# A new order of block two's projection, its indexer columns first, and 28 unit turns ahead of seven norms

## The chip, the cores and the metric

The kernel runs as one program on one core of a Trainium2 chip. The metric is the device time of one execution in microseconds, the median of three runs; beside it stands one profiled execution. The engines are TensorE (PE, its weight loads are PEld), VectorE (DVE), ScalarE (ACT), GpSimd (POOL) and SyncE (SP), which issues the loads from DRAM. Each runs its own list of instructions in order and waits for the others by semaphores. Matmuls write to eight banks of PSUM, each of 512 f32 columns; the other engines read them from there.

## The reference

Two transformer blocks of two layers each work on 256 rows of width 1024, in f32. Block one (attention with a context of 256 rows, a Fourier mix, a gated unit, then a squared-ReLU MLP) is not changed, apart from turns added ahead of three of its norms. Block two's attention is what the tables reorder:

```python
h = rms_norm_2(x, attn_norm_g[l])
proj = h @ w_in[l]
(mq, mk, mv, dq, dk, dv, sq, sk, sv, iq, ik, iw) = jnp.split(proj, offsets, axis=-1)
moba = moba_attention(qk(mq, MOBA_HEADS, qg[0]), qk(mk, MOBA_HEADS, kg[0]), split_heads(mv, MOBA_HEADS))
dq_h = qk(dq, 2 * DIFF_HEADS, qg[1])
dk_h = qk(dk, 2 * DIFF_HEADS, kg[1])
...
diff = diff_attention(dq_h[:, 0::2], dq_h[:, 1::2], dk_h[:, 0::2], dk_h[:, 1::2],
                      split_heads(dv, DIFF_HEADS), lam)
diff = rms_norm_2(diff, diff_subln_g[l]) * (1.0 - lam_init)
iq_h = apply_rope(split_heads(iq, IDX_HEADS), cos, sin)
ik_r = apply_rope(ik, cos, sin)
dsa = dsa_attention(qk(sq, DSA_HEADS, qg[2]), qk(sk, DSA_HEADS, kg[2]),
                    split_heads(sv, DSA_HEADS), iq_h, ik_r, iw * (IDX_HEADS ** -0.5))
mix = jnp.concatenate([merge_heads(moba), merge_heads(diff), merge_heads(dsa)], axis=-1)
x = x + mix @ w_out[l]
h2 = rms_norm_2(x, ffn_norm_g[l])
x = x + (jax.nn.silu(h2 @ w_gate[l]) * (h2 @ w_up[l])) @ w_down[l]
```

Here `qk` is a norm over each head of 64 and a rotation (rope). With 256 rows, moba is plain causal attention with 4 heads; differential attention has 4 heads with two score maps each; the sparse attention (dsa) keeps for each query the 64 best causal keys by an indexer score, a weighted sum over 8 heads of relu(iq . ik).

## The kernel before

**Weights.** Every weight passes through slots of 128 x 1024 f32. SP loads a slot into one of 8 raw buffers (`put`, from L706); ScalarE casts it to the rounded type fp32r (L962, `w_hi`), VectorE subtracts to get the rest (L1270, `w_lo`), and PE multiplies it in three matmuls, hi x hi, hi x lo and lo x hi (`three`, L1762). SP may be 8 slots ahead, the casts and splits 4. Activations are split in the same way.

**Norms.** Ahead of a projection VectorE and ScalarE norm the rows, PE turns them (a transpose, a matmul against the unit matrix) into PSUM (`turn_x` in block one, `norm2` in block two, L1867), VectorE and ScalarE write the halves `act_hi` and `act_lo`, and PE starts on the projection. There are eight such norms, the first at the program's start. PE has nothing else to do in them.

**Block two's projection** (`rows2`, L2167) runs over eight blocks of columns in the order of `BLOCKS2`: dq, dk (differential queries and keys, 512 columns each), iq (indexer queries, 512), dv (512), ik (72 columns: the indexer's 64 key columns and 8 weights, one slot with all 8 tiles of k), mqk, sqk (queries and keys of moba and of dsa) and mv_sv (256 columns of moba's values and 256 of dsa's, fetched by two loads a slot). All but ik have four slots with two tiles of k, so there are 29 slots or steps. Behind each step all engines look in the table `FILL2` and do what stands there for this step; behind the slots of the output projection `out2` (8 slots, `down`, L2085) they look in `OUT2`. The entries are:

- ("drain", j, t): ScalarE copies row tile t of block j out of PSUM, with squares for the head norms where there are any.
- ("first", r), ("second", r), ("turn", r): unit r is 256 columns of rotated heads. VectorE does the head norm's sum and the rope in the first half; POOL makes the power -1/2; VectorE scales in the second; PE turns the result in four matmuls (L1908) into bank 2.
- ("score", j), ("weigh", j), ("mix", j): step j of 16 attention steps. PE's scores with the mask (L2033, L2036), then VectorE's maximum (L1586), ScalarE's exponential and VectorE's division (L1597 to L1604); PE turns the probabilities (L2047, "weigh") and multiplies by the values (L2068, "mix"). Steps 0 to 7 are differential (group 0 and 1), 8 to 11 moba (group 2), 12 to 15 dsa (group 3).
- ("logits", g): PE's indexer logits (into bank 2), ScalarE's relu, VectorE's weighted sum. ("search", t, n): n of the 8 rounds (L1730, L1731) in which VectorE finds the 64 best keys of row tile t, eight a round; the last round also writes the mask `seen` (L1734, L1735), without which PE can't score group 3.
- ("square" and "norm", t), ("turn_rows", t): the norm of the differential result, then its turning by PE (L2080).

The table is written by hand: nothing moves by itself, and each engine takes its part of an entry in the table's order. Bank 2 is shared by the units' turns, the logits and the turned rows; `turn_bank` waits for its last reader.

Of the kernel before, what the change touches and what calls it, by code (L numbers as in the profile page):

```python
# [14 lines left out]
P = 128  # L15
D = 1024
KT = D // P
# [8 lines left out]
SPLIT2, MIXES = 6, 6  # L26
W = 512
# [70 lines left out]
def build(nc, A, consts, out, n):  # L98
    top = ExitStack()
    with top:  # L100
# [76 lines left out]
        with ExitStack() as s:  # L177
# [106 lines left out]
        BLOCKS2 = (("dq", DQ), ("dk", DK), ("iq", IQ), ("dv", DV), ("ik", IK), ("mqk", MQ), ("sqk", SQ), ("mv_sv", MV))  # L284
# [38 lines left out]
            4: [("first", 0)],  # L323
            5: [("second", 0), ("first", 1), ("turn", 0)],
            6: [("second", 1), ("turn", 1)],
            7: [("drain", 1, 0), ("drain", 1, 1)],
            8: [("first", 2)],
            9: [("second", 2), ("first", 3), ("turn", 2)],
            10: [("second", 3), ("turn", 3)],
            11: [("drain", 2, 0), ("drain", 2, 1), ("score", 0)],  # L330
            12: [("weigh", 0), ("first", 4), ("second", 4), ("score", 1)],
            13: [("weigh", 1), ("first", 5), ("second", 5), ("score", 2)],
            14: [("weigh", 2), ("turn", 4), ("score", 3)],
            15: [("drain", 3, 0), ("weigh", 3), ("drain", 3, 1), ("turn", 5), ("score", 4)],
            16: [("weigh", 4), ("mix", 0), ("mix", 1), ("drain", 4, 0), ("drain", 4, 1), ("score", 5)],
            17: [("weigh", 5), ("mix", 2), ("mix", 3), ("first", 6), ("second", 6), ("index_scale",), ("turn", 6), ("score", 6)],
            18: [("weigh", 6), ("mix", 4), ("logits", 0), ("logits", 1), ("score", 7)],
            19: [("weigh", 7), ("mix", 5), ("mix", 6), ("logits", 2)],
            20: [("drain", 5, 0), ("drain", 5, 1), ("mix", 7), ("logits", 3)],
            21: [("logits", 4), ("first", 7), ("square", 0)],  # L340
            22: [("logits", 5), ("second", 7), ("first", 8), ("turn", 7), ("square", 1)],
            23: [("second", 8), ("turn", 8), ("norm", 0), ("search", 0, 2)],
            24: [("drain", 6, 0), ("drain", 6, 1), ("search", 0, 3), ("norm", 1), ("turn_rows", 0), ("score", 8)],
            25: [("weigh", 8), ("search", 0, 3), ("turn_rows", 1), ("first", 9), ("score", 9)],
            26: [("weigh", 9), ("second", 9), ("first", 10), ("turn", 9), ("score", 10)],
            27: [("weigh", 10), ("second", 10), ("turn", 10), ("search", 1, 2), ("score", 11)],
            28: [("drain", 7, 0), ("weigh", 11), ("drain", 7, 1), ("search", 1, 1), ("score", 12)],
        }
        OUT2 = {
            0: [("weigh", 12), ("mix", 8), ("mix", 9), ("search", 1, 2), ("score", 13)],  # L350
            1: [("weigh", 13), ("mix", 10), ("mix", 11), ("search", 1, 3), ("score", 14)],
            2: [("weigh", 14), ("score", 15)],
            3: [("weigh", 15), ("mix", 12), ("mix", 13)],
            4: [("mix", 14)],
# [132 lines left out]
        def units2(l):  # L487
            out_ = []
            for name, c, p0, g, q in (("dq", DQ, 4, 2, 1), ("dq", DQ + 256, 6, 2, 1), ("dk", DK, 8, 3, 0), ("dk", DK + 256, 10, 3, 0),
# [1789 lines left out]
```

## Time and profile before

| what | value |
|---|---|
| median of three runs | 1750.43 us (1750.07 to 1750.53) |
| the profiled execution | 1748.0 us |
| its span, first to last instruction | 1745.9 us |
| busy PE, VectorE, ScalarE, POOL | 1614.8, 1049.1, 731.8, 99.2 us |
| mean granted clock of PE | 0.965 |
| read from DRAM | 255.15 MB, 147 GB/s over the span |
| chain that ended last | PE 81%, VectorE 11%, issue 3%, ScalarE 2% |

The span's times start at its first instruction. The granted clock is given as a share: 1.00 is 2.4 GHz, 0.50 is 1.2 GHz. Busy times of PE are modelled: matmuls overlap, so the distance from one start to the next is the better price of one in a row. Block one takes the span up to 964, block two's first layer from there to 1356, the second the rest.

### The profile page before, as it was taken

The numbers are of one execution on the slowest core, as the hardware profiler recorded it, in microseconds if no ns is written. First come the engines' busy times: TensorE is split into PE (matmuls) and PEld (weight loads), VectorE is DVE, ScalarE is ACT, GpSimd is POOL, SyncE is SP. The second block draws the span as 40 slices with busy tenths as digits, with TensorE's granted clock in tenths as the row PEclk, the third lists the DMA queues.
The fourth block names the chain that finished last, engine by engine and source line by source line (L and its number), as shares of the span: only waits on it lengthen the run. The fifth ranks groups of instructions, "written<-read, shape, count | busy, mean of one in ns | idle before, by whom it ended". The sixth has DMA issues, their size and how long they took to land.

```text
span 1745.9 us, 22902 instructions
## 1 busy us (share of the span) xinstructions
PE 1614.8 (92%) x9050; PEld 1309.9 (75%) x9050; DVE 1049.1 (60%) x1599; ACT 731.8 (42%) x1246; POOL 99.2 (6%) x88
## 2 busy tenths in 40 slices
PE   6999889999999989989999897789999887789999
PEld 3865676788888866569988675579998666579997
DVE  3537654533443356666644867758874767768873
ACT  3425523421342224635533544444443444444542
POOL 1010000000000001000000301000000201000000
PEclk9999999999999989999999989899999999899999
DMA  9348224432333324848666632246656432246653
GB/s 358 111 154 312 101 89 135 131 96 89 94 97 95 97 72 133 290 131 268 182 191 184 173 108 83 67 122 183 187 185 189 134 109 83 72 124 186 185 183 119
DMA packets 174218, 257.69 MB, mean 148 GB/s; under 512 B 10448, under 2 KB 92640, under 8 KB 173984
## 3 DMA queue, kind: packets, MB, share of 16 engines
q1 hardware_dynamic: 171872, 250.38, 45.9%
q0 software_dynamic: 2016, 5.77, 1.3%
q8 instruction: 72, 1.18, 0.3%
q14 instruction: 34, 0.28, 0.1%
q10 hardware_dynamic: 224, 0.07, 0.0%
HBM read 255.15 MB, written 1.05 MB: 147 GB/s over the span
## 4 chain that ended last, share of the span: by engine, by line
PE 81%; DVE 11%; issue 3%; ACT 2%; DMA 1%; POOL 1%; SPq 0%; POOLq 0%; DVEq 0%; ACTq 0%
PE bank L1764 49%; PE pair_bank L1764 20%; DVE w_lo L1270 2%; PE bank L1816 2%; PE bank L2015 1%; PE pair_bank L1987 1%; PE pair_bank L2033 1%; PE bank L1998 1%; DVE wide L1354 1%; PE bank L1928 1%; DVE rope_a L1420 1%; POOL xrstd L848 1%; DVE head_sq L1428 1%; DMA raw<-in_w_ada 1%; DVE proj L1448 1%
## 5 line engine op out<-in xcount | busy, mean ns | idle before, releaser
L1270 DVE TENSOR_TENSOR w_lo<-raw,w_hi 128x1024 fp32r<-128x1024 f32 x374 | 450.1, 1219 | 304.8 <-ACT w_hi L962 301.9
L962 ACT CAST w_hi<-raw 128x1024 fp32r<-128x1024 f32 x374 | 386.7, 1044 | 391.1 <-PE bank L1764 315.2
L1764 PE MATMUL pair_bank<-act_hi,w_hi 128*128 128x256 f32 (+1 forms) x736 | 230.4, 313 | 9.9 <-DVE act_lo L1344 4.5
L1764 PE MATMUL pair_bank<-act_hi,w_lo 128*128 128x256 f32 (+1 forms) x736 | 227.0, 308 | 0.0
L1764 PE MATMUL pair_bank<-act_lo,w_hi 128*128 128x256 f32 (+1 forms) x736 | 226.8, 308 | 0.0
L1764 PE MATMUL bank<-w_hi,act_hi 128*128 128x512 f32 (+2 forms) x528 | 218.2, 413 | 4.2 <-DVE w_lo L1270 2.2
L1764 PE MATMUL bank<-w_hi,hid_lo 128*128 128x512 f32 x560 | 221.4, 395 | 0.0
L1764 PE MATMUL bank<-w_hi,hid_hi 128*128 128x512 f32 x560 | 221.3, 395 | 0.0
L1764 PE MATMUL bank<-w_lo,hid_hi 128*128 128x512 f32 x560 | 221.3, 395 | 0.0
L1764 PE MATMUL bank<-w_lo,act_hi 128*128 128x512 f32 (+2 forms) x528 | 209.8, 397 | 0.0
L1764 PE MATMUL bank<-w_hi,act_lo 128*128 128x512 f32 (+2 forms) x528 | 208.9, 396 | 0.0
L1764 PEld LDWEIGHTS pair_bank<-act_hi,w_hi 128*128 128x128 f32 x736 | 140.2, 190 | 25.2 <-DVE act_lo L1344 7.8
L1764 PEld LDWEIGHTS pair_bank<-act_lo,w_hi 128*128 128x128 f32 x736 | 140.2, 190 | 7.4 <-issue 1.0
L1764 PE MATMUL bank<-act_hi,w_hi 128*128 128x256 f32 (+1 forms) x480 | 145.0, 302 | 0.6 <-DVE w_lo L1270 0.6
L1764 PEld LDWEIGHTS pair_bank<-act_hi,w_lo 128*128 128x128 f32 x736 | 140.2, 191 | 7.0
L1764 PE MATMUL bank<-act_hi,w_lo 128*128 128x256 f32 (+1 forms) x480 | 144.3, 301 | 0.0
L1764 PE MATMUL bank<-act_lo,w_hi 128*128 128x256 f32 (+1 forms) x480 | 144.3, 301 | 0.0
L1764 PEld LDWEIGHTS bank<-w_hi,act_hi 128*128 128x128 f32 x528 | 106.9, 202 | 27.6 <-issue 3.4
L1764 PEld LDWEIGHTS bank<-w_hi,hid_lo 128*128 128x128 f32 x560 | 105.1, 188 | 25.4
L1764 PEld LDWEIGHTS bank<-w_hi,hid_hi 128*128 128x128 f32 x560 | 105.2, 188 | 25.3
L1764 PEld LDWEIGHTS bank<-w_lo,hid_hi 128*128 128x128 f32 x560 | 105.1, 188 | 25.3
L1764 PEld LDWEIGHTS bank<-w_hi,act_lo 128*128 128x128 f32 x528 | 105.4, 200 | 21.7
(227 smaller groups left out, 2103.9 us busy)
## 6 DMA issues: line engine op xcount, KB each, us to landing
raw<-in_w_mlp SPq DMA_DIRECT2D x128, 512.0 KB, 3.7
raw<-in_w_ada SPq DMA_DIRECT2D x96, 512.0 KB, 5.7
raw<-in_w_in SPq DMA_DIRECT2D x72, 512.0 KB, 3.6
raw<-in_w_gate SPq DMA_DIRECT2D x44, 512.0 KB, 3.7
raw<-in_w_up SPq DMA_DIRECT2D x44, 512.0 KB, 3.7
raw<-in_w_down SPq DMA_DIRECT2D x44, 512.0 KB, 3.5
raw<-in_w_out SPq DMA_DIRECT2D x32, 512.0 KB, 3.8
raw<-in_w_in SPq DMA_DIRECT2D x16, 256.0 KB, 3.0
```

The source lines that it names most:

```text
L848: nc.gpsimd.tensor_tensor(xrstd[:, m, g:g + 1], xvar[:, m, g:g + 1], neg_half[:, 0:1], ALU.pow).then_inc(xrstd_ready, 1)
L962: nc.scalar.copy(hi_of(i)[:, 0:w], raw[:, i % RAW, 0:w]).then_inc(hi_ready, 1)
L1270: nc.vector.tensor_tensor(w_lo[:, i % RAW, 0:w], raw[:, i % RAW, 0:w], hi_of(i)[:, 0:w].bitcast(F32), ALU.subtract).then_inc(lo_ready, 1)
L1354: nc.vector.tensor_scalar(wide[:, (2 * k + s) % 4, :], b[:, (k % 2) * NT:(k % 2 + 1) * NT], mscale[:, which, k, s:s + 1], mod[:, 24 * whic ...
L1420: nc.vector.tensor_tensor(t1, x, u["cos"].unsqueeze(2).broadcast_to([P, TT, heads, DH]), ALU.mult).then_inc(dve_order, 1)
L1428: ins = nc.vector.tensor_tensor(t2[:, :, :, lo:lo + wd], x[:, :, :, other:other + wd], sin[:, :, lo:lo + wd].unsqueeze(2).broadcast_to([P, ...
L1448: ins = nc.vector.tensor_tensor(d, t1, f, ALU.mult) if u["normed"] else nc.vector.tensor_tensor(d, t1, t2, ALU.add)
L1764: ins = nc.tensor.matmul(o, a[x], b[y], start=first and i == 0, stop=True, skip_group_check=True)
L1816: ins = nc.tensor.matmul(bank[bk][j:j + 32, :], cond[:, k, :], tiles(raw[:, r, :], 2)[:, kk, :], start=k < 4, stop=True, skip_group_check= ...
L1928: ins = nc.tensor.matmul(bank[5][:], proj1[:, 2 * s + t, F1 + i * P:F1 + (i + 1) * P], dft_n[:, t, :], start=t == 0, stop=t == TT - 1)
L1987: nc.tensor.matmul(bank[a][:, 0:w], st["q"][a], st["k"][a], start=True, stop=True).then_inc(scored, 1)
L1998: ins = nc.tensor.matmul(st["o"][a], st["v"][a][kt], probs_t1[:, j % 2, a, kt, :], start=kt == 0, stop=kt == keys - 1)
```

## The change

There are two edits, independent of each other.

**The order.** `BLOCKS2` starts with the indexer queries, then comes a new block mv_ik of 328 columns (moba's 256 values and the indexer's 72 columns) in three slots of 3, 3 and 2 tiles of k, and the last block sv holds only dsa's 256 values, in two slots of 4 tiles. There are 29 slots as before. `FILL2` and `OUT2` are written anew for this order: the indexer's units, the logits and the search start earlier, the attention steps later (the first score stands behind step 17 in place of step 11, the last behind slot 3 of the output projection in place of 2), and the steps come closer together. The units are renumbered, indexer first (`units2`), the banks of the output projection are swapped to fit (`down_bank`), and the buffers of the casts rotate over six from block two's first slot on (`hi_of`, `hi_before`).

**The turns.** `keep_busy` issues 28 turns of the unit matrix into bank 7, which nobody reads, on PE alone. It is called ahead of the turns of `norm2` (four times in a run), of `rows1` in layer 1, and of `up1`'s first slot in layers 0 and 1.

```diff
-SPLIT2, MIXES = 6, 6
+SPLIT2, MIXES, BUSY = 6, 6, 28
...
-        BLOCKS2 = (("dq", DQ), ("dk", DK), ("iq", IQ), ("dv", DV), ("ik", IK), ("mqk", MQ), ("sqk", SQ), ("mv_sv", MV))
+        BLOCKS2 = (("iq", IQ), ("mv_ik", IK), ("dq", DQ), ("dk", DK), ("dv", DV), ("mqk", MQ), ("sqk", SQ), ("sv", SV))
...
-            11: [("drain", 2, 0), ("drain", 2, 1), ("score", 0)],
-            12: [("weigh", 0), ("first", 4), ("second", 4), ("score", 1)],
...
+            24: [("weigh", 6), ("mix", 5), ("second", 7), ("square", 0), ("first", 8), ("turn", 7), ("score", 7)],
+            28: [("drain", 7, 0), ("weigh", 10), ("mix", 9), ("drain", 7, 1), ("second", 9), ("first", 10), ("norm", 1), ("turn", 9), ("score", 11)],
...
         OUT2 = {
-            0: [("weigh", 12), ("mix", 8), ("mix", 9), ("search", 1, 2), ("score", 13)],
...
+            0: [("weigh", 11), ("mix", 10), ("second", 10), ("turn_rows", 0), ("turn", 10), ("turn_rows", 1), ("score", 12)],
...
         def down_bank(key, gs, ch, g):
             if key == "out2":
-                return bank[(4, 2, 5, 3)[2 * ch + g - 2]]
+                return bank[(4, 5, 3, 2)[2 * ch + g - 2]]
...
-            return [(j, name, c, 1 if name == "ik" else 4, KT if name == "ik" else 2, IN2 - IK if name == "ik" else W)
-                    for j, (name, c) in enumerate(BLOCKS2)]
+            shape = dict(mv_ik=(256 + IN2 - IK, (3, 3, 2)), sv=(256, (4, 4)))
+            return [(j, name, c, *shape.get(name, (W, (2, 2, 2, 2)))) for j, (name, c) in enumerate(BLOCKS2)]
...
+                        if name == "mv_ik":
+                            self.put("w", nk * wd, lambda r: [(tiles(r[:, 0:nk * wd], nk)[:, :, 0:256], src[:, ks, MV:MV + 256]),
+                                                              (tiles(r[:, 0:nk * wd], nk)[:, :, 256:wd], src[:, ks, IK:IN2])])
...
-                        if t == 0 and u["r"] >= 2:
+                        if t == 0:
                             self.e.wait_ge(rows_ready, n.at("rows_ready", us[u["r"] - 2]["key"]))
...
+            def keep_busy(self):
+
+                if 7 in self.ada_before:
+                    self.e.wait_ge(mod_ready, n.at("mod_ready", self.ada_before[7]))
+                for i in range(BUSY):
+                    nc.tensor.transpose(bank[7][:, i % 4 * P:(i % 4 + 1) * P], ident, ident)
...
             def norm2(self, m, l, which):
                 e = self.e
+                self.keep_busy()
...
+                if l:
+                    self.keep_busy()
                 for s in both if l else ():
                     self.turn_x(m, both, s, 0)
...
+                        if (h, j, q) == (0, 0, 0):
+                            self.keep_busy()
...
                 if key == "out2":
                     e.wait_ge(drained, n.at("drained", ("rows2", l, 6, 1)))
-                    self.turn_bank()
...
-                        if key == "out2" and ch and j == start:
-                            e.wait_ge(drained, n.at("drained", ("rows2", l, 7, g - 2)))
+                        if key == "out2" and j == start:
+                            if (ch, g) in ((0, 3), (1, 2)):
+                                e.wait_ge(drained, n.at("drained", ("rows2", l, 7, ch)))
+                            elif ch:
+                                self.turn_bank()
```

**Order of instructions.** On PE ahead of block two's first norm, before (`hid` is the last projection of block one, `xn` the normed rows, `const` the unit matrix):

```order
L1764 MATMUL bank<-w_lo,hid_hi 128x512
L1764 MATMUL bank<-w_hi,hid_lo 128x512
L1867 MATMUL pair_bank<-const,xn 128x128 [waits xn_ready]
L1867 MATMUL pair_bank<-const,xn 128x128 x7
L1867 MATMUL bank<-const,xn 128x128 x4
L1867 MATMUL pair_bank<-const,xn 128x128 [waits norm_lo]
L1867 MATMUL pair_bank<-const,xn 128x128 x3
L1764 MATMUL bank<-w_hi,act_hi 128x512 [waits norm_lo,lo_ready]
```

and after:

```order
L1762 MATMUL bank<-w_lo,hid_hi 128x512
L1762 MATMUL bank<-w_hi,hid_lo 128x512
L1826 MATMUL bank<-const 128x128 [waits mod_ready]
L1826 MATMUL bank<-const 128x128 x27
L1873 MATMUL pair_bank<-const,xn 128x128 [waits xn_ready]
L1873 MATMUL pair_bank<-const,xn 128x128 x7
L1873 MATMUL bank<-const,xn 128x128 x4
L1873 MATMUL pair_bank<-const,xn 128x128 [waits norm_lo]
L1873 MATMUL pair_bank<-const,xn 128x128 x3
L1762 MATMUL bank<-w_hi,act_hi 128x512 [waits norm_lo,lo_ready]
```

The 28 turns stand between the last matmul of the MLP and the wait for the normed rows; the norm's own turns and their waits are the same.

On PE in block two's layer 0, where the indexer's keys are projected, before (behind an attention step's turned probabilities, a unit's turns and the next step's scores):

```order
L2047 MATMUL bank<-const,probs 128x128 [waits prob_ready,prob_t]
L1908 MATMUL bank<-const,proj 128x128 [waits rows_ready,turned_out]
L1908 MATMUL bank<-const,proj 128x128 x3
L2033 MATMUL pair_bank<-pairs_t 128x256 [waits exped,turned_out]
L2033 MATMUL pair_bank<-pairs_t 128x256
L2036 MATMUL pair_bank<-mask_b,ident_b 128x128 x2
L1764 MATMUL bank<-w_hi,act_hi 128x72 [waits drained,lo_ready]
L1764 MATMUL bank<-w_lo,act_hi 128x72
L1764 MATMUL bank<-w_hi,act_lo 128x72
```

and after, behind the last slot of iq:

```order
L1762 MATMUL bank<-w_lo,act_hi 128x512
L1762 MATMUL bank<-w_hi,act_lo 128x512
L1762 MATMUL bank<-w_hi,act_hi 128x328 [waits lo_ready]
L1762 MATMUL bank<-w_lo,act_hi 128x328
L1762 MATMUL bank<-w_hi,act_lo 128x328
```

The matmuls of 72 columns are gone; 48 of 328 columns stand right behind the first block, with no attention between.

On VectorE in layer 0's output projection, from the split of the slot ahead of attention step 13's weighing to the first of the three search rounds behind it, before:

```order
L1270 TENSOR_TENSOR w_lo<-raw,w_hi 128x1024 [waits hi_ready]
L1597 RECIPROCAL total<-total 128x2 [waits exped]
L1603 TENSOR_TENSOR probs<-probs,total 128x2x128 [waits dve_order]
L1484 TENSOR_TENSOR act_lo<-bank,act_hi 128x2x256 [waits mix_hi]
L1730 MAX best<-score 128x8
L1731 MATCH_REPLACE score<-best,score 128x256 [waits dve_order]
L1730 MAX best<-score 128x8 [waits dve_order]
```

and after:

```order
L1268 TENSOR_TENSOR w_lo<-raw,w_hi 128x1024 [waits hi_ready]
L1595 RECIPROCAL total<-total 128x2 [waits exped]
L1601 TENSOR_TENSOR probs<-probs,total 128x2x128 [waits dve_order]
L1728 MAX best<-score 128x8
L1729 MATCH_REPLACE score<-best,score 128x256 [waits dve_order]
L1728 MAX best<-score 128x8 [waits dve_order]
```

The lower half of mixed rows (L1484, now L1482) no longer stands between the weighing and the search. In both, two more rounds, the mask and then the maximum of score 14 follow.

## Rows read from the trace of the kernel before

**Rows 1.** Page, part 1: busy time of PE and PEld, share of span, instructions.

```profile
PE 1614.8 (92%) x9050; PEld 1309.9 (75%) x9050; DVE 1049.1 (60%) x1599; ACT 731.8 (42%) x1246; POOL 99.2 (6%) x88
```

**Rows 2.** Stretches around norms: stretch and length, busy (count) by engine, clock, DMA, GB/s.

```profile
255.20:258.90 3.70, 3.65 (x17) 3.68 (x18) 3.24 (x9) 1.62 (x4) 0.00 (x0) 0.50 0.21 64
258.90:262.00 3.10, 2.36 (x11) 1.46 (x11) 3.10 (x9) 1.63 (x4) 0.00 (x0) 1.00 0.00 0
628.00:632.10 4.10, 0.00 (x0) 0.00 (x0) 3.77 (x14) 1.45 (x4) 2.35 (x4) 0.86 0.37 128
632.10:644.60 12.50, 10.39 (x37) 8.54 (x38) 8.62 (x19) 3.25 (x8) 0.79 (x1) 0.50 0.00 0
...
768.10:770.90 2.80, 2.74 (x12) 2.42 (x12) 1.60 (x5) 0.81 (x2) 0.03 (x1) 0.50 0.32 94
964.60:970.20 5.60, 0.00 (x0) 0.00 (x0) 4.52 (x10) 1.70 (x5) 3.47 (x4) 0.88 0.32 97
970.20:975.70 5.50, 5.41 (x21) 4.96 (x22) 4.00 (x6) 3.48 (x6) 4.88 (x9) 0.50 0.70 121
...
1162.90:1166.80 3.90, 3.65 (x16) 3.18 (x16) 2.82 (x4) 1.89 (x4) 0.59 (x1) 0.50 0.39 134
```

**Rows 3.** Same view: keys block of layer 0, then block two's stretch of each layer.

```profile
1033.80:1044.00 10.20, 10.20 (x41) 8.55 (x41) 2.94 (x6) 2.57 (x8) 0.00 (x0) 0.50 0.18 51
...
973.60:1158.00 184.40, 158.88 (x768) 121.37 (x766) 128.10 (x270) 86.92 (x198) 21.47 (x13) 0.90 0.37 109
1364.30:1545.00 180.70, 154.71 (x768) 117.40 (x766) 126.19 (x262) 85.69 (x195) 19.97 (x10) 0.93 0.35 103
```

**Rows 4.** Waits of PE in 1364.3 to 1545: total us, times, longest.

```profile
PE bank L1908 <- DVE proj L1448: 6.4, 4, 3.7
PE bank L2047 <- DVE probs L1603: 5.5, 2, 3.3
```

**Rows 5.** PE in order of time, block two's layer 1: start, length, what.

```profile
1406.05 0.27 PE L2047 MATMUL bank<-const,probs 128*128 128x128 f32 x1
...
1518.75 1.22 PE L2033 MATMUL pair_bank<-pairs_t 64*128 64x256 f32 x4 [5.07 <-issue]
...
1528.12 0.63 PE L2047 MATMUL bank<-const,probs 128*128 128x128 f32 x4
```

**Rows 6.** PE in order of time, turns of the norm in layer 0.

```profile
255.25 4.16 PE L1854 MATMUL bank<-const,xn 128*128 128x128 f32 x20 [0.56 <-DVE xn L1329]
...
266.89 1.03 PE L1854 MATMUL bank<-const,xn 128*128 128x128 f32 x8
```

**Rows 7.** Chain that ended last: start, length, what, number of matmuls.

```profile
639.00 6.65 PE bank L1764 x21
647.52 4.09 PE bank L1764 x21
...
1030.60 7.21 PE bank L1764 x48
...
1179.80 11.47 PE bank L1764 x96
...
1420.62 5.34 PE bank L1764 x48
...
1525.34 2.75 PE bank L1764 x12
```

**Rows 8.** VectorE in order of time, block two's layer 1.

```profile
1466.66 0.68 DVE L1414 TENSOR_REDUCE variance<-head_sq 128x8 f32<-128x512 f32 x1
...
1469.66 1.22 DVE L1270 TENSOR_TENSOR w_lo<-raw,w_hi 128x1024 fp32r<-128x1024 f32 x1
1470.80 0.69 DVE L1448 TENSOR_TENSOR proj<-rope_a,rstd 128x512 f32<-128x512 f32 x1
...
1504.79 0.42 DVE L1730 MAX8 best<-score 128x8 f32<-128x256 f32 x1
...
1505.76 0.43 DVE L1730 MAX8 best<-score 128x8 f32<-128x256 f32 x1
```

More of the change, by code:

```diff
@@ L332, in build @@
[L332 to L347, printed above, removed]
+            4: [("first", 0), ("second", 0)],
+            5: [("first", 1), ("second", 1), ("turn", 0)],
+            6: [("drain", 1, 0), ("drain", 1, 1), ("turn", 1)],
@@ new lines, in build @@
+            7: [("first", 2), ("second", 2), ("index_scale",), ("turn", 2), ("logits", 0)],
+            8: [("logits", 1)],
+            9: [("logits", 2)],
+            10: [("drain", 2, 0), ("drain", 2, 1), ("logits", 3)],
+            11: [("first", 3), ("logits", 4)],
+            12: [("second", 3), ("first", 4), ("turn", 3)],
+            13: [("second", 4), ("turn", 4), ("logits", 5)],
+            14: [("drain", 3, 0), ("drain", 3, 1), ("search", 0, 3)],
+            15: [("first", 5), ("search", 0, 1)],
@@ new lines, in build @@
+            16: [("second", 5), ("first", 6), ("turn", 5)],
+            17: [("second", 6), ("turn", 6), ("score", 0)],
+            18: [("drain", 4, 0), ("weigh", 0), ("drain", 4, 1), ("search", 0, 2), ("score", 1)],
+            19: [("weigh", 1), ("mix", 0), ("search", 0, 2), ("score", 2)],
+            20: [("weigh", 2), ("mix", 1), ("search", 1, 1), ("score", 3)],
+            21: [("weigh", 3), ("mix", 2), ("search", 1, 1), ("score", 4)],
+            22: [("drain", 5, 0), ("weigh", 4), ("mix", 3), ("drain", 5, 1), ("score", 5)],
@@ new lines, in build @@
+            23: [("weigh", 5), ("mix", 4), ("first", 7), ("score", 6)],
+            24: [("weigh", 6), ("mix", 5), ("second", 7), ("square", 0), ("first", 8), ("turn", 7), ("score", 7)],
+            25: [("weigh", 7), ("mix", 6), ("second", 8), ("turn", 8), ("norm", 0), ("score", 8)],
+            26: [("drain", 6, 0), ("weigh", 8), ("mix", 7), ("drain", 6, 1), ("search", 1, 1), ("score", 9)],
+            27: [("weigh", 9), ("mix", 8), ("first", 9), ("square", 1), ("score", 10)],
+            28: [("drain", 7, 0), ("weigh", 10), ("mix", 9), ("drain", 7, 1), ("second", 9), ("first", 10), ("norm", 1), ("turn", 9), ("score", 11)],
@@ L348, in build @@
         }
         OUT2 = {
-            0: [("weigh", 12), ("mix", 8), ("mix", 9), ("search", 1, 2), ("score", 13)],
[L351 to L354, printed above, removed]
+            0: [("weigh", 11), ("mix", 10), ("second", 10), ("turn_rows", 0), ("turn", 10), ("turn_rows", 1), ("score", 12)],
+            1: [("weigh", 12), ("mix", 11), ("search", 1, 2), ("score", 13)],
@@ L355, in build @@
+            2: [("weigh", 13), ("search", 1, 3), ("mix", 12), ("score", 14)],
+            3: [("weigh", 14), ("mix", 13), ("score", 15)],
+            4: [("weigh", 15), ("mix", 14)],
             5: [("mix", 15)],
@@ L2025, in score @@
                 e, key, w = self.e, st["key"], st["keys"] * P
-                u = units2(key[1])[(3, 3, 8, 10)[st["group"]]]
+                u = units2(key[1])[(6, 6, 8, 10)[st["group"]]]
                 e.wait_ge(turned_out, n.at("turned_out", u["key"]))
@@ L2170, in rows2 @@
                 step = 0
-                for j, name, c, ns, nk, wd in rows2_blocks():
-                    for q in range(ns):
+                for j, name, c, wd, slots in rows2_blocks():
+                    k0 = 0
+                    for q, nk in enumerate(slots):
                         w = self.take(nk)
@@ L2208, in logits @@
                 if g == 0:
-                    for u in units2(l)[4:7]:
+                    for u in units2(l)[0:3]:
                         self.e.wait_ge(turned_out, n.at("turned_out", u["key"]))
```

53 lines of the change are left out of this document (21 added, 32 removed).

## The prediction

> **What bounds the kernel now.** I read first the page's engine table: PE is busy for 92% of the span [rows 1], so a gain must come from PE doing less, idling less, or running less of its work at its lower clock. The stretch table (busy time and granted clock of each engine) is read next, once around the norms and once over block two's projection and attention, which the new tables reorder. What the reader is to see there: a norm leaves PE without work for 4.1 to 5.6 us, and the work behind it then runs at a granted clock of 0.50, the 1.2 GHz level [rows 2]. This happens at seven norms. Block two's two stretches take 184.4 and 180.7 us with PE recorded busy for 158.9 and 154.7 and at mean clocks of 0.90 and 0.93 [rows 3]; VectorE is busy for 128.1 and 126.2 in them. There the two engines hand work to each other, and neither alone is the limit. The list of waits and the order of time tell who is late for whom [rows 4, 5].
>
> **Part 1, the unit turns.** Seven times, PE gets 28 turns of the unit matrix into bank 7 ahead of a norm's turns. Their only wait, on the last reader of bank 7, was met long before. Eight turns back to back take 1.03 us at the full clock and 20 take 4.16 at the lower one [rows 6], so 0.11 to 0.13 and 0.21 each. The 28 start when PE has just finished dense matmuls at the full clock: 28 x 0.11 to 0.13 = 3.1 to 3.6 us. The shortest gap is 4.1 us [rows 2], so they delay nothing; that gap is their cover, and with less than 3.1 us of it each missing microsecond would be paid in full. What they buy is the clock. From each norm I count only what lies on the chain:
> - Second norm of block one, layer 0: VectorE's scaling paces it; only the first turns come earlier. 0.4 us.
> - First norm of layer 1: the cold stretch from 632.1 is 12.5 us long [rows 2]. In it 21 matmuls take 6.65 us, and the same 21 one group later take 4.09 at the full clock [rows 7]: 2.6 us, and 0.6 from the turns. 3.2 us.
> - Second norm of layer 1 (768.1), and the last one at 1549.8 which is like it: cold for 2.8 us only [rows 2]. 0.6 and 0.8.
> - Block two's first norm: the 5.5 us from 970.2 hold 5.41 of PE work [rows 2]. 12 turns ahead of the first matmul save 1.2 us (16 x 0.1, less what ScalarE and VectorE pace), and five wide matmuls at 0.43 against 0.23 save 1.0. 2.2 us.
> - The norm at 1158 and the one at 1356: turns at half price ahead of VectorE's four subtractions. 1.0 and 1.3.
> The sum is 9.5 us. From below: 0, if the clock falls all the same. From above: the seven cold stretches are some 36 us long (five of them in [rows 2]), nearly all PE's own work, and the full clock would halve that: 16 us, since a part is paced by VectorE. I take 9.5, since VectorE's rows of 0.4 to 0.7 us stand between the turns and the matmuls and do not get faster. The weakest place is the 5.6 us gap at 964.6: behind 3.1 us of turns 2.5 us stay empty.
>
> A rule speaks against this part, and the rows answer it. The stretch from 255.2 to 258.9 holds nothing on PE but turns, and the next row's clock is 1.00 [rows 2]: these f32 turns alone brought it back. The Trainium skill, "TensorE: Matmul & The Clock Gate", section "Part 4: PE-mode transpose", says that the full rate does not engage for transposes, since they do not count as PE being busy in the same way. By that rule part 1 would be worth 0 and not 9.5 us; by the row it holds.
>
> **Part 2, narrow matmuls.** Before, the indexer's keys are a block of their own: 48 matmuls of 72 columns, 5.34 us in layer 1 and 7.21 in layer 0 [rows 7]. PE's clock falls behind them in both layers; in layer 0 the whole stretch from 1033.8 to 1044.0 is at 0.50 with PE busy for all 10.2 us [rows 3]. Now these columns ride with 256 of moba's values: 48 matmuls of 328 columns, and the other values are 48 of 256 in place of 48 of 512. 96 of 256 columns take 11.47 us, 0.1195 each, and 12 of 512 take 2.75, 0.229 each [rows 7]; between them 328 columns come to 0.150. Before: 5.34 + 48 x 0.229 = 16.3. After: 48 x 0.150 + 48 x 0.1195 = 12.9. It saves 3.4 us a layer (bounds 2 and 5), and in layer 0 another 4, about half of the 10.2 cold ones with what VectorE hid taken off. Bytes, slots (29) and casts are the same in sum; the two-piece loads go from 8 to 6 a layer.
>
> **Part 3, the order.** All prices are pitches of layer 1's rows (a few small ones were read from the same lists in order of time and have no row here). VectorE: a split 1.14, a unit's first half 3.0, its second 0.6 [rows 8]; a search round 0.97 over 256 keys [rows 8], 0.7 over 128. PE: a slot 2.75, a unit's four turns 0.45, a score 0.65 or 0.85, a group of logits 1.07. From the end of one step's weighing on VectorE to the end of the next I take the larger of two paths: PE's small work and its slot, or VectorE's work between weighing and scoring and then maximum, split and weighing, 2.4 us for 128 keys and 3.05 for 256 (2.0 and 2.5 without lambda).
> - To the first weighing. Before: 1364.7 to 1406.05 [rows 5], 41.4 us with 13 slots. After: 10.9 us for four slots; then the indexer's units cost no wait (their halves, 1.4 and 0.6, fit beside slots), the logits hide behind slots at 3.8 a step, and the normed units of dq and dk come where VectorE is the later one. Walking them through, PE waits 2.5, 1.5, 3.4 and 1.5 for second halves: 71.3 us with 19 slots.
> - From first to last weighing. Before: 1406.05 to 1528.12 [rows 5], 122.1 us. After, the fifteen intervals are 3.8, 4.3, 3.9, 4.5, 4.5, 5.9, 8.1 (a first half behind ScalarE's squares), 5.4, 4.5, 5.5, 6.7, 8.4 (two turnings of the differential rows and one unit's turns, all through bank 2, one behind another), 6.2, 7.3 (three search rounds ahead of the score that needs them) and 4.4: 83.4 us.
> - Behind it: 16.8 us before, 12.6 after.
> The sum is 167.3 us at the full clock against 180.3. The clock will fall again where PE idles: behind the wait for dk's second half, at the 8.1 us interval, at step 28 with the one behind it (12 us, no slot inside), and at the search's end. A slot at the lower clock costs 2.4 us more; three or four, partly hidden, are 5.5 us. So layer 1 saves about 7.5, and that holds part 2's 3.4; layer 0 saves 4 more, 11.5. The first norm's 1.0 us of matmuls is counted twice, so 18 for both. Bounds: 0 a layer if the walk's idle times come twice as long, and 15 and 19 if they vanish into the slots' slack. The queues that steps pass: POOL's powers need 1.7 to 2 us and are asked for a whole step ahead; SP's loads stand 8 slots ahead; ScalarE in step 22 has two drains of 1.4 ahead of its exponentials and adds 0.6 us.
>
> The 5.07 us wait for the search in each layer [rows 5] does not go: the new table still has three rounds and a mask, 3.7 us, ahead of that score, with 0.5 of PE work beside them. It shrinks to about 3.
>
> **Sum.** 9.5 + 18 = 27.5. The profiled execution's 1748.0 (span 1745.9) becomes 1720.5 (span 1718.4), and the shown runs' median, 1750.43, which is 2.4 above it, becomes 1723.
>
> **Rivals.**
> - *The order frees more.* For: PE's list shows 6.4 and 5.5 us of waits for VectorE [rows 4], both of kinds that the new order thins out. Against: VectorE's own sum from step 11 to the search's end is 95 us by these prices and PE's 88, so PE cannot run ahead. 15 + 19 + 9.5 - 1 gives 1708.
> - *The order frees nothing.* VectorE, being the later engine from step 11 on, eats part 2's gain, and only the norms and layer 0's clock are left: 9.5 + 3, 1738.
> - *The turns do not hold the clock.* 18 alone remain: 1732. Against it stands the row at 258.9; for it, the wide gap at 964.6 and the turns' own idle tail.
> - *Slower.* From step 23 to the third slot of the output projection VectorE's path exceeds PE's in nearly every interval. If the clock falls there and stays down, nine slots a layer cost 2.4 us more each, 21.6, of which VectorE's lateness hides about 5. The place is these nine slots; it decides from the point where more than 15.5 us a layer are uncovered, that is eight or nine cold slots. 2 x 16.5 = 33 over the forecast: 1756. Against: behind the norms, where PE stands empty for longer, the low stretches end by themselves after 2.8 to 12.5 us [rows 2].
> The change does do what it says: the order of instructions shows all seven runs of 28 turns and 48 matmuls of 328 columns a layer.
>
> **How the numbers follow.** Forecast (1713 to 1735) 0.50; more freed 0.16; nothing freed 0.13; clock not held 0.11; slower 0.06; the rest, 0.04, at no change. No change means within 0.2%, 3.5 us, about what can be told apart here: 1746.9 to 1753.9. Faster 0.90, same 0.04, slower 0.06. The range reaches over both neighbours on the fast side and to the weaker gains: 1703 to 1742.
>
> **What would show it.** Seven stretches of turns, each 3.1 to 3.6 us, with a clock of 1.00 over the first 5 us behind each norm; the 21 matmuls of layer 1's first block in 4.1 us; 18 matmuls of 328 columns in 2.7 us, and no fall of the clock behind them; PE's first weighing 71 us behind the start of block two's stretch, the last 83 behind that; the wait for the search near 3 us. The prediction is wrong if the turns run at 0.21 each, if the clock reads 0.50 behind a norm, or if PE's waits for second halves pass 15 us a layer.

## The result, and the profile after

The changed kernel takes 1738.38 us (median of four runs, 1737.77 to 1738.93), the kernel before 1750.48 in four runs (1750.07 to 1751.96). The ratio is 0.9928, with a 95% interval of 0.9913 to 0.9944: faster by 12.1 us, where 27.5 was forecast. The profiled execution takes 1738.16 us with a span of 1736.2, so 9.8 us less than the profiled one of before.

The engine table of the page has PE busy for 8 us more than before [rows 1]. The 196 unit turns add 22.5 us, so the rest of PE's work is recorded with 14 us less:

```profile
PE 1623.1 (93%) x9246; PEld 1319.1 (76%) x9246; DVE 1048.3 (60%) x1599; ACT 730.8 (42%) x1246; POOL 95.2 (5%) x88
```

The stretch table around the norms (columns as in [rows 2]; the first row of a norm is the time of its 28 turns):

```profile
248.20:251.40 3.20, 3.19 (x29) 2.95 (x27) 3.01 (x12) 1.45 (x4) 1.27 (x3) 1.00 0.54 163
254.50:257.90 3.40, 3.40 (x19) 3.40 (x18) 3.12 (x8) 1.71 (x5) 0.00 (x0) 0.52 0.17 51
...
633.40:643.60 10.20, 8.32 (x30) 6.82 (x29) 6.36 (x17) 3.24 (x8) 0.00 (x0) 0.51 0.01 2
...
765.50:770.90 5.40, 2.73 (x19) 2.12 (x18) 4.17 (x11) 1.26 (x4) 1.54 (x2) 1.00 0.20 55
...
967.90:971.30 3.40, 3.37 (x17) 3.30 (x18) 2.40 (x3) 1.71 (x3) 3.40 (x7) 0.52 0.64 103
1151.50:1154.70 3.20, 3.17 (x29) 2.93 (x27) 2.43 (x6) 1.12 (x4) 1.69 (x2) 1.00 0.58 189
1154.70:1161.00 6.30, 2.50 (x18) 2.05 (x19) 5.39 (x7) 3.10 (x5) 0.99 (x2) 1.00 0.25 84
```

The turns take 3.2 us a norm, as costed. Behind the norms at 768, 1158, 1356 and 1545 of before the clock now stays at 1.00 (the rows at 765.5 and 1154.7 are two of them). Behind the others it still falls: for 3.4 us at 254.5 and 967.9, and for 10.2 at 633.4, where it was 12.5 [rows 2].

Then the block of 328 columns in layer 0, block two's projection and attention of each layer (columns as in [rows 3]), and the three long low stretches of layer 1:

```profile
982.00:989.60 7.60, 7.60 (x53) 7.56 (x52) 7.37 (x11) 3.99 (x5) 0.00 (x0) 1.00 0.65 189
971.20:1151.50 180.30, 153.72 (x769) 117.17 (x768) 127.81 (x271) 86.39 (x198) 19.49 (x13) 0.91 0.36 113
1356.10:1535.80 179.70, 152.39 (x770) 116.03 (x769) 125.93 (x261) 84.95 (x194) 17.95 (x10) 0.92 0.34 105
1466.20:1473.10 6.90, 6.29 (x20) 4.83 (x21) 2.06 (x4) 3.43 (x9) 0.00 (x0) 0.51 0.01 2
1490.10:1500.40 10.30, 7.97 (x35) 5.55 (x34) 3.17 (x6) 3.75 (x9) 0.00 (x0) 0.51 0.01 2
1510.60:1517.40 6.80, 5.43 (x16) 3.92 (x17) 3.76 (x9) 1.95 (x5) 0.00 (x0) 0.51 0.00 0
```

Measured from the first matmul of the projection to the last of the output projection, layer 0 takes 180.3 us where it took 184.3, and layer 1 takes 179.7 where it took 180.4. Summed over PE's own time list, from the last matmul ahead of a norm to the first behind it, the seven norms take 61.7 us where they took 65.7. So 4.0 us come from the norms, 4.0 from layer 0's attention and 0.7 from layer 1's; 1.0 more lies ahead of the norm at 250, where nothing was changed. The changed kernel was profiled once more in the experiments: there layer 0 takes 180.3 us again and layer 1 takes 180.9, and the seven norms take 60.4. So layer 1's 0.7 is less than two profiles of one kernel differ by.

PE in order of time in layer 1 (start, length, what, idle time before it and what ended it), the weighings (L2055) of steps 7, 8, 11, 12 and 13 and the scores of step 14 (L2041):

```profile
1464.85 0.41 PE L2055 MATMUL bank<-const,probs 128*128 128x128 f32 x2 [3.26 <-DVE probs L1599]
...
1472.95 0.38 PE L2055 MATMUL bank<-const,probs 128*128 128x128 f32 x2
...
1489.78 0.91 PE L2055 MATMUL bank<-const,probs 128*128 128x128 f32 x4 [4.20 <-DVE probs L1604]
...
1501.96 0.38 PE L2055 MATMUL bank<-const,probs 128*128 128x128 f32 x2
...
1508.40 0.41 PE L2055 MATMUL bank<-const,probs 128*128 128x128 f32 x2 [2.04 <-DVE probs L1601]
...
1511.97 1.22 PE L2041 MATMUL pair_bank<-pairs_t 64*128 64x256 f32 x4 [2.79 <-issue]
```

Each of the three low stretches begins in or just behind such a wait: 3.26 us of emptiness ahead of 1464.85, 4.20 ahead of 1489.78, 2.04 and 2.79 ahead of 1508.40 and 1511.97. The walk of part 3 had 8.1, 5.4, 4.5, 5.5, 6.7, 8.4, 6.2, 7.3 and 4.4 us for the last nine intervals between weighings. Measured are 8.2, 8.1, 4.7, 5.5, 6.6, 12.2, 6.4, 9.6 and 4.7. Three are too long, by 2.7, 3.8 and 2.3 us, and they are the three that hold a low stretch.

### The profile page after: what moved, and what is told of

It is laid out like the page before. It is cut to its first block, busy times and chain, and to the rows that moved or that the text cites. A ratio compares the mean times of both kernels' runs of the same rounds, so it can differ in the third digit from the quotient of the medians.

```text
span 1736.2 us, 23296 instructions
## 1 busy us (share of the span) xinstructions
PE 1623.1 (93%) x9246; PEld 1319.1 (76%) x9246; DVE 1048.3 (60%) x1599; ACT 730.8 (42%) x1246; POOL 95.2 (5%) x88
## 4 chain that ended last, share of the span: by engine, by line
PE 80%; DVE 12%; issue 2%; ACT 2%; DMA 2%; POOL 1%; SPq 0%; POOLq 0%; DVEq 0%; ACTq 0%
PE bank L1762 48%; PE pair_bank L1762 20%; DVE w_lo L1268 2%; PE bank L1814 2%; DMA raw<-in_w_ada 1%; PE bank L2023 1%; PE pair_bank L1995 1%; PE bank L2006 1%; DVE wide L1352 1%; PE bank L1936 1%; POOL xrstd L846 1%; DVE neg_max L1584 1%; PE pair_bank L2041 1%; DVE rope_a L1437 1%; DVE rope_a L1418 1%
## 5 line engine op out<-in xcount | busy, mean ns | idle before, releaser
L1268 DVE TENSOR_TENSOR w_lo<-raw,w_hi 128x1024 fp32r<-128x1024 f32 (+2 forms) x374 | 450.1, 1219 | 297.4 <-ACT w_hi L960 294.8
L960 ACT CAST w_hi<-raw 128x1024 fp32r<-128x1024 f32 (+2 forms) x374 | 386.7, 1044 | 383.3 <-PE bank L1762 308.6
L1762 PE MATMUL bank<-w_hi,act_hi 128*128 128x512 f32 (+2 forms) x528 | 213.1, 404 | 3.4 <-DVE act_lo L1342 2.1
L1762 PE MATMUL bank<-w_lo,act_hi 128*128 128x512 f32 (+2 forms) x528 | 205.6, 389 | 0.0
L1762 PE MATMUL bank<-w_hi,act_lo 128*128 128x512 f32 (+2 forms) x528 | 204.6, 387 | 0.0
```

The source lines that it names most:

```text
L960: nc.scalar.copy(hi_of(i)[:, 0:w], raw[:, i % RAW, 0:w]).then_inc(hi_ready, 1)
L1268: nc.vector.tensor_tensor(w_lo[:, i % RAW, 0:w], raw[:, i % RAW, 0:w], hi_of(i)[:, 0:w].bitcast(F32), ALU.subtract).then_inc(lo_ready, 1)
L1762: ins = nc.tensor.matmul(o, a[x], b[y], start=first and i == 0, stop=True, skip_group_check=True)
```

## The experiments

There are twelve experiments in three groups of four, each group on another chip; two of them repeat a kernel. The kernel before had medians of 1750.65, 1749.70 and 1751.28 us there, so the groups can be compared within about 1 us.

**The two edits alone.** The first has the new order and no turns, the second the old order with the turns:

```diff
-SPLIT2, MIXES, BUSY = 6, 6, 28
+SPLIT2, MIXES, BUSY = 6, 6, 0
...
             def keep_busy(self):
+                if not BUSY:
+                    return
```

> The changed kernel without the 28 turns ahead of the norms: the order alone. Theory (additive): the two traces put 4.0 us of the gain at the seven norms and 4.7 in block two's two stretches (4.0 in layer 0, 0.8 in layer 1), 1.0 in front of the first norm, where nothing was changed; so without the turns the time is 4 over the changed kernel, 1742 to 1743, with the seven low clock stretches back. Rival: the turns also help the stretches behind the norms, and the order alone gives less than half of the gain, above 1745. Other rival: the turns give nothing, 1738.

> The kernel before with the 28 turns ahead of the seven norms and nothing else. Theory: 4 us less than before, 1746.5, with the low clock gone behind four norms (768, 1158, 1356, 1545) and shortened to one stretch of 3.4 us at 253 and 968, while layer 1's first block (633) gains nothing. Rival, by the prediction's sum: 9.5 us less, 1741.

The order alone took 1745.6 us (12 runs, 1737.81 to 1748.19; ratio 0.9977, interval 0.9962 to 0.9992), the turns alone 1748.7 (12 runs, 1741.6 to 1754.46; ratio 0.9987, interval 0.9969 to 1.0005). So the order gives 5.1 us; the turns alone give 2.0, which can't be told from nothing, though the interval does exclude the 9.5 of the prediction's sum. The first theory had 1742 to 1743 for the order alone and missed by 3 us; the rival, above 1745 and less than half of the gain, has the measured time. Its profiled execution is 6.9 us over the changed kernel's, and the norms hold 3.1 of that: 2.5 stand in the two layers' attention (in layer 1 low stretches of 34 us in sum where the changed kernel has 27) and 1.9 behind the last norm, where a low stretch of 10.2 us stands. The two parts together give 7.1 us where the changed kernel has 12.1, or 10.1 when measured again; what the other 3 to 5 us are is not shown. With the turns alone the seven norms do take 4.2 us less in its profile, but the five stretches behind them in which the change does nothing are 0.5 to 1.1 us longer each, 3.8 in all.

**Turns in the attention's waits.** PE issues unit turns where it waits, into a bank that it is about to write anyway, ahead of the wait:

```diff
+            def hold(self, b, count):
+                for i in range(count):
+                    nc.tensor.transpose(bank[b][:, i % 4 * P:(i % 4 + 1) * P], ident, ident)
...
+                if j:
+                    e.wait_ge(exped, n.at("exped", (key, j - 1, 1)))
+                if j == 14:
+                    self.hold(0, 22)
                 if st["group"] == 3:
                     e.wait_ge(seen_ready, n.at("seen_ready", (key[1], st["keys"] - 1)))
-                if j:
-                    e.wait_ge(exped, n.at("exped", (key, j - 1, 1)))
...
                     e.wait_ge(prob_t, n.at("prob_t", (key, j - 1)))
+                self.hold(6, {6: 9, 7: 26, 10: 8, 11: 34, 13: 16}.get(j, 0))
                 e.wait_ge(prob_ready, n.at("prob_ready", (key, j)))
...
                 u = units2(l)[r]
+                if r == 10:
+                    self.hold(0, 12)
```

Ahead of the scores PE's two waits change places, so that the turns of step 14 stand behind the one and ahead of the other.

> The changed kernel with more unit turns in block two's attention, in the time in which PE waits there: ahead of the weighing of steps 6, 7, 10, 11 and 13 (9, 26, 8, 34 and 16 turns into bank 6), 22 ahead of the scores of step 14 and 12 ahead of the last unit's turns (into bank 0). Theory (the clock takes the gain): the three intervals of layer 1 that came out too long, 8.1, 12.2 and 9.6 us against 5.4, 8.4 and 7.3, all hold slots at the low clock; with PE busy they fall to about 5.4, 8.4 and 7.3, so 9 us a layer less, 1720 to 1724. Rival (VectorE and ScalarE are the later ones there and hide the slow slots): within 2 us of the changed kernel, 1736 to 1740, though the clock reads 1.00. Third case: the turns don't hold the clock or stand in the way, above 1740.

It took 1722.36 us (6 runs, 1721.59 to 1727.69; ratio 0.9845, interval 0.9821 to 0.9870), and 1723.26 when it ran again on the third chip:

> The kernel of the held attention unchanged, as the yardstick on the chip of these runs: 1722 to 1723.

The stretch table of the first of them, block two's attention in each layer:

```profile
971.00:1143.00 172.00, 158.88 (x895) 124.31 (x894) 127.78 (x270) 86.25 (x198) 20.01 (x14) 0.99 0.40 118
...
1349.20:1520.60 171.40, 158.00 (x896) 123.93 (x895) 125.86 (x261) 84.85 (x194) 17.96 (x10) 0.99 0.37 110
```

Both layers are 8.3 us shorter than in the changed kernel, at a clock of 0.99 in place of 0.91 and 0.92. VectorE's busy time did not change. The last nine intervals between weighings are now 8.2, 5.4, 4.7, 5.4, 6.6, 9.1, 6.4, 7.4 and 4.7 us. The rival is refuted: VectorE hides little of the slow slots. The clock took 8.3 us a layer, and with it held none of these intervals differs from the walk's by more than 0.7.

**One place left open.** Does the clock answer to the one wait, or to the stretch as a whole? Against the kernel with all turns:

```diff
-                self.hold(6, {6: 9, 7: 26, 10: 8, 11: 34, 13: 16}.get(j, 0))
+                self.hold(6, {6: 9, 7: 26, 10: 8, 11: 0, 13: 16}.get(j, 0))
...
                 if r == 10:
-                    self.hold(0, 12)
+                    self.hold(0, 0)
```

> The kernel of the held attention without its turns at one place: none ahead of the weighing of step 11 (34) and none ahead of the last unit's turns (12); the other places stay. Theory (the idle time itself lets the clock fall, at the place where it stands): only the interval between the weighings of steps 11 and 12 grows, from 9.1 us to 11.5 to 13.5, with a low stretch of 7 to 14 us behind step 11, the others stay within 0.3 us; two layers, 5 to 8 us more, 1728 to 1730. Rival (the clock answers to the whole stretch's work, not to one wait): low stretches come back at other intervals too, above 1732, or nowhere, 1722.

It took 1729.83 us (1725.18 to 1731.09), 6.6 over its neighbour with all turns. In its profile only the interval behind step 11 grows, from 9.1 to 12.5 us (13.2 in layer 0); all others of the last nine stay within 0.1. PE in order of time, and the stretch table of the low stretch there:

```profile
1483.33 1.09 PE L2063 MATMUL bank<-const,probs 128*128 128x128 f32 x4 [4.26 <-DVE probs L1604]
```

```profile
1480.80:1494.50 13.70, 8.84 (x37) 6.37 (x38) 5.26 (x11) 5.15 (x13) 0.00 (x0) 0.51 0.01 1
```

A single wait of 4.3 us, with the chain of small work through bank 2 behind it, costs 13.7 us at the low clock and 3.4 us of time in this layer, 4.1 in layer 0. The run does not part the 4.3 us from the waits of 1.6 and 0.8 us in that chain, which lost 12 turns too.

**Half as many turns.** The counts are 4, 13, 4, 17, 8, then 11 and 6, in place of 9, 26, 8, 34, 16, then 22 and 12.

> The kernel of the held attention with about half as many turns at each of its places (4, 13, 4, 17, 8 ahead of the weighings, 11 ahead of the scores of step 14, 6 ahead of the last unit's turns), so that 1 to 2 us of each wait stay empty. Theory (a short wait is not enough to let the clock fall): still 1722 to 1726. Rival (the gain goes with the turns' share): half of it, 1730.

It took 1727.92 us (1723.6 to 1731.07). Its profiled execution (1723.6) has attention stretches of 172.0 and 172.2 us, as good as with all turns; in it the clock falls once more, at step 11 of layer 1, for 3.4 us, and that interval is 9.9 us in place of 9.1. The other executions were slower by up to 7.5 us, at mean clocks of 0.981 to 0.984 where the profiled one has 0.986, with no profile that would say where. The median lies between the two expectations. So half the turns held the clock in the profiled execution, and in the others less well.

**The old order with the same help.** What is the order worth once neither loses the clock? The kernel before gets the turns ahead of the norms and its own turns in its attention waits (`hold`, `keep_busy` and the two waits ahead of the scores as above):

```diff
+                self.hold(6, {7: 16, 9: 26, 12: 17}.get(j, 0))
...
+                if j == 14:
+                    self.hold(0, 42)
...
+                if r in (6, 7):
+                    self.e.wait_ge(exped, n.at("exped", (self.steps[0]["key"], 5 if r == 6 else 7, 1)))
+                    self.hold(0, 14 if r == 6 else 30)
...
             def diff_turn(self, l, t):
                 e = self.e
+                if t == 0:
+                    self.hold(0, 19)
```

> The kernel before, so the old order, with the 28 turns ahead of the seven norms and with more unit turns in its own attention, where its PE waits 1.9 to 5.1 us: 14 and 30 ahead of two units' turns, 19 ahead of the first turned rows, 16, 26 and 17 ahead of the weighing of steps 7, 9 and 12, 42 ahead of the scores of step 14. It tells what the order is worth once neither order loses the clock; with the clock held the new order's stretches took 172.0 and 171.4 us. Theory (the order itself is worth the difference of the narrow matmuls and some of the waits): some 177 and 175 us, the sum 1729 to 1733. Rival (the clock was all): 172 in both layers, 1720 to 1724. Other rival (the order is worth the full 13 us a layer of the walk): above 1738.

It took 1735.05 us (1731.42 to 1736.67; ratio 0.9919, interval 0.9899 to 0.9939). The stretch table:

```profile
973.30:1150.90 177.60, 166.39 (x933) 130.18 (x932) 128.09 (x271) 86.87 (x198) 21.76 (x14) 0.98 0.38 113
1357.10:1534.10 177.00, 166.25 (x933) 130.30 (x932) 126.14 (x261) 85.44 (x194) 19.99 (x10) 0.98 0.35 105
```

The stretches came out 0.6 and 2.0 us over the theory's 177 and 175, the time 2 us over its range. So with the waits filled the new order is worth 5.6 us in each layer (177.6 against 172.0, 177.0 against 171.4). It is an upper figure: the old order still has a low stretch in each layer, which begins among the matmuls of the indexer's keys:

```profile
1034.50:1041.30 6.80, 6.80 (x26) 5.35 (x26) 2.54 (x6) 2.54 (x8) 0.00 (x0) 0.50 0.27 77
...
1416.80:1423.60 6.80, 6.80 (x30) 5.73 (x30) 1.04 (x2) 0.93 (x4) 0.00 (x0) 0.50 0.28 80
```

The new one has 3.4 us at the low clock in each layer, so up to 1.7 of the 5.6 can be the clock's (an estimate, half of the 3.4 us that the old order has more). The clock costs the old order 6.7 us in layer 0 and 3.4 in layer 1, and the new one 8.3 in each. With these figures the two layers of the change read so: 5.6 less 1.6 is the 4.0 of layer 0, and 5.6 less 4.9 the 0.7 of layer 1. Each figure is of one profile, and profiles of one kernel differ by up to 1.3 us in such a stretch.

**More at the norms, less at the norms.** Three kernels vary the turns there. The first has more of them in front:

```diff
+                self.site = getattr(self, 'site', -1) + 1
-                for i in range(BUSY):
+                for i in range((37, 37, 40, 49, 43, 43, 43)[self.site]):
```

> The changed kernel with 37, 37, 40, 49, 43, 43 and 43 turns in place of 28, so that PE is busy nearly up to the first normed row at each of the seven norms (0.115 us a turn against gaps of 4.4, 4.4, 4.8, 5.8 and 5.1 us). Theory (the remaining idle time of 1.2 to 2.6 us behind the turns is what still lets the clock fall at 254, 633 and 968): the low stretch at 968 goes and 1.2 us with it, those at 254 and 633 go or stay by the waits of 1.0 and 1.4 us between the turns; together 1 to 4 us less, 1734 to 1737. Rival: the length of the turns in front doesn't matter, same time within 1 us.

It took 1739.08 us, no change: the rival's case. Its norms take 1.7 us less than the changed kernel's, and the low stretch at 968 is gone, but two new ones stand a few us behind other norms. The same two stand in the kernel with the held attention, here from its stretch table:

```profile
771.10:774.50 3.40, 3.40 (x17) 3.40 (x18) 0.83 (x2) 0.43 (x2) 0.00 (x0) 0.53 0.00 0
...
1153.30:1156.70 3.40, 3.40 (x19) 3.40 (x18) 1.13 (x1) 0.00 (x0) 0.00 (x0) 0.52 0.00 0
```

They lie on dense matmuls: the stretches that hold them are 194.1 us long against 192.7, and 189.4 against 187.9. A low stretch there costs 1.4 to 1.5 us of its 3.4, while the turns gained 0.5 and 0.9 at these two norms. So a clock that is held over a norm can fall right behind it and take more than was won. The second kernel has the turns in the attention and none at the norms:

> The kernel of the held attention (new order, turns in block two's waits), without the 28 turns ahead of the seven norms. Theory: the norms cost 3 to 4 us as in the order alone against the changed kernel, 1726 to 1727. Rival: with the attention held, the norms' low stretches stand alone and the turns are worth the 7 us that the order alone lacked, 1729 to 1730.

It took 1727.97 us (1726.26 to 1731.88), 4.7 to 5.6 over the kernel with the turns ahead of the norms, between the two expectations. Here, with the attention held, the turns at the norms are worth what the theory said and a little more. The third has the first one's counts in front, the turns in the attention, and more:

> The kernel of the held attention with more turns at the norms: 37, 37, 40, 49, 43, 43 and 43 in front, and 8, 8 and 14 between the turns of block one's norms, where PE waits 1.0 to 1.8 us more. Theory: the low stretches at 255, 638 and 969 go, 2 to 5 us less, 1717 to 1720. Rival, by the run with more turns in front: the low stretch comes a few us later, behind the norm, and the time is the same within 1 us.

With 8, 8 and 14 further turns between those of block one's norms it took 1720.36 us (5 runs, 1716.07 to 1725.78; ratio 0.9829, interval 0.9807 to 0.9851), against 1723.26 beside it. This is the lowest median of all, 18 us under the changed kernel, but its runs overlap those of the kernel beside it (1721.45 to 1723.77). Its stretch table at two of the three norms where the 28 turns had not been enough:

```profile
627.80:640.00 12.20, 10.50 (x87) 9.46 (x86) 11.72 (x30) 4.12 (x11) 3.14 (x4) 1.00 0.16 44
960.60:971.00 10.40, 9.54 (x75) 8.71 (x74) 8.63 (x15) 4.80 (x10) 8.08 (x12) 1.00 0.49 97
```

The clock is 1.00 through both, and the stretch behind the norm at 633 is 123.3 us long where it was 125.9: here are 2.5 of the 3.2 us that the prediction had put there. Not all of it is owed to the added turns. The 21 matmuls of that block on the chain that ended last (start, length), in the changed kernel's first profile, in its second, and here:

```profile
637.97 6.60 PE bank L1762 x21
```

```profile
638.92 5.60 PE bank L1762 x21
```

```profile
638.99 4.08 PE bank L1762 x21
```

With the same 28 turns the second profile has a low stretch of 3.4 us there in place of 10.2, and the stretch behind the norm is 1.0 us shorter. The kernel with the held attention, beside this one, has 5.83 us for the 21.

**More in the attention.** Against the kernel with the held attention, turns ahead of three more units:

```diff
-                if r == 10:
-                    self.hold(0, 12)
+                self.hold(0, {3: 14, 4: 10, 5: 27, 10: 12}.get(r, 0))
```

> The kernel of the held attention with turns also ahead of the turns of units 3, 4 and 5 (14, 10 and 27 into bank 0), where PE waits 1.8, 1.3 and 3.3 us and one low stretch of 3.4 us a layer is left (at 1023 and 1412). Theory (a low stretch costs up to half its length): 1 to 3 us less, 1719 to 1721. Rival (VectorE hides it, or the turns push the low stretch elsewhere): the same within 1 us.

It took 1724.73 us (1724.09 to 1726.3), not better than 1722.36 and 1723.26, and a little over what the rival said: the theory of 1 to 3 us less is wrong. Layer 0 took 171.5 us with no low stretch, layer 1 172.7 with one of 3.4 us that had moved to 1419.1, onto slots.

**The yardstick.**

> The changed kernel unchanged, on the chip of these runs. By every theory 1738 to 1739; it is the yardstick for the others, and shows whether its runs scatter as little as with the first measurement (1737.8 to 1738.9), while the kernel before scattered from 1743.2 to 1754.9 on the second chip.

It took 1739.65 us (1737.37 to 1741.49). That is 1.3 over the first measurement, with 10.1 us between it and the kernel before beside it.

## Why the prediction was wrong

- **The unit turns' own price** was right: 3.2 us for 28, inside the gap, nothing delayed.
- **That turns alone hold the clock** was right at four norms of seven; at the other three the clock read 0.51 or 0.52 behind the norm, which the prediction had named as a sign of being wrong. The rows at 1151.5 and 1154.7 hold, up to the first matmul at 1160.7, nothing on PE but the unit turns and the norm's own, and read 1.00. The prediction weighed the rule that transposes do not count for the full rate (the Trainium skill, "TensorE: Matmul & The Clock Gate", "Part 4: PE-mode transpose"). By these rows it does not hold for these f32 turns, which the kernel issues with `nc.tensor.transpose` and the trace lists as MATMUL without a mode. The rival *the turns do not hold the clock* had named the right weak place, the gap at 964.6.
- **What the norms give** is a term of the sum that was mis-sized: 9.5 us forecast, 4.0 measured, 5.3 in the second profile, which wins 1.0 more behind the norm at 633 and loses 1.4 behind the one at 768. First the 3.2 us at layer 1's first norm. In the first profile the low stretch there began later and ended at the same piece of work, and the same 21 matmuls took 6.60 us where they took 6.65 [rows 7]; in the second they took 5.60. The 4.1 that the prediction expected came only when turns filled the waits between the norm's own turns as well (4.08). Second the 2.2 at block two's first norm, of which 0.8 came: behind the turns 2.6 us stayed empty and the clock fell.
- **The narrow matmuls** were right: in layer 0's row at 982 above, the 48 of 328 columns and four turns of a unit take 7.6 us at a clock of 1.00; less 0.45 for the turns that is 0.149 each, against 0.150. The 48 of 256 columns take 5.9 us in the kernel with the held attention, against 5.7. Layer 0 gained 3.3 us more than layer 1, where 4 had been forecast.
- **The order at the full clock** is the step that failed most: "The sum is 167.3 us at the full clock against 180.3." That is 13.0 us a layer; with the waits filled in both orders it is at most 5.6, of which about 3.3 are the narrow matmuls (16.3 before, 7.2 and 5.9 now). Two faults make the difference. The walk was 4.1 us short in layer 1: 71.3, 83.4 and 12.6 us against 73.0, 85.4 and 13.0 with the held clock, 167.3 against 171.4, in many small shares and one low stretch that was left. And the 180.3 of before was no full-clock figure: it held its own loss by the clock, 3.4 us in layer 1, as the old order with turns showed.
- **The clock in the attention** is the other step that failed: "A slot at the lower clock costs 2.4 us more; three or four, partly hidden, are 5.5 us." All four places were named rightly: behind dk's second half (1408), at the 8.1 us interval, at step 28, at the search's end, where the wait came out at 2.8 us as forecast. The size was not. It is 8.3 us, of which 2.7, 3.1 and 2.2 stand in the three intervals. Three or four slots at 2.4 are 7.2 to 9.6, so the fault is the deduction for what is hidden. PE is busy for 19.7 us in the three long low stretches; half of that, 9.8 us, is what they would cost with nothing hidden (an estimate), so 1.5 us or so was hidden. The waits that let the clock fall were in the walk's own intervals, and the prediction gave them one common term where each needed its own.

So of the 19 us forecast for the two layers' attention (18 without the double count), 4.7 came. Of the 14.3 that are missing, the walk has 4.1 a layer and the clock 2.8 a layer, 13.8 together; the rest is layer 0's 4 us that came out as 3.3. So the walk has the larger part of what is missing in the attention; the norms lack another 5.5 us. The rival *the order frees nothing*, 1738, has the measured time, but not for its reason: VectorE did not eat the gain of the narrow matmuls; with the clock held the new order takes 8.3 us less a layer. That the sum of other misses comes to the rival's number is chance. The chance of faster was right.

## What to carry to other kernels

Where PE waits for several us inside a stretch of dense work, price the wait twice: its own length, and the work behind it at half clock, on the path, for each such wait by itself. An order that packs the work closer but leaves PE the same few long waits gives part of its gain back to the clock; filling exactly these waits with unit turns into a bank that is about to be written lengthened none of the last nine intervals here and brought 16 us, more than the reordering. Compare orders at the same clock, since a measured stretch of before already holds its own loss.

## What was not expected of the hardware

Some kernels scatter far more than others. The kernel before had runs from 1742.6 to 1755.4 us in 43 runs on the three chips of the experiments, though its first four had lain within 1.9 us. The kernel with held attention had nine of its ten runs from 1721.4 to 1723.8 and one at 1727.7. The changed kernel, in ten runs of two chips, lay from 1737.4 to 1741.5. The time at the low clock does not put them in order: the kernel with more turns in front of the norms alone, at a mean clock of 0.976 in its profile, had six runs within 1.5 us, and the fastest kernel, at 0.990, five runs from 1716.1 to 1725.8. Profiled executions of the same code at these spots differ in where a low stretch stands: the changed kernel had none at 771 in its first profile, and in its second, on another chip, one of 3.4 us at 772, with the stretch that holds it 1.45 us longer. What decides this from one execution to the next stays open. It also sets a bound for single profiles: a difference of 1 to 2 us in one stretch can be where the clock fell, and nothing else.
